# Mixture-of-experts weights as whole 128-wide stationary tiles, with the hidden units dealt out four neighbours to a partition

## What is computed

```python
def moe_swiglu(h, w_router, b_router, w_gate, w_up, w_down):   # 8 experts, D_FF_EXPERT = 3584
    logits = t @ w_router + b_router
    top_v, top_e = lax.top_k(logits, 2)
    gate = softmax(top_v)
    ...
    def one(args):
        xb, e = args
        return (silu(xb @ w_gate[e]) * (xb @ w_up[e])) @ w_down[e]
    out = lax.map(one, (xr, blk_e))
    y = zeros.at[row_tok].add(out * row_g)
```

## Time and profile before

| | |
|---|---|
| median of 3 runs | 2288.18 us (2286.75 to 2290.34) |
| the profiled execution: its own time / its span | 2291.82 us / 2290.1 us |
| PE, DVE, ACT, POOL busy, share of the span | 97%, 39%, 17%, 7% |
| mean granted TensorE clock | 0.985 of full speed |
| read from HBM | 532.94 MB |
| the experts' stretch of PE | 858 to 1743 us |

### The profile page before, as it was taken

One profiled execution on the slowest core, in us unless ns is written; L12 is line 12 of the kernel. 1 busy time (PEld: TensorE's weight loads), 2 busy tenths in 40 slices (PEclk: granted clock), 3 DMA queues, 4 the chain that ended last, 5 costly groups with the idle time before them and its releaser, 6 DMA issues. The chain is left out here.

```text
span 2290.1 us, 49032 instructions
## 1 busy us (share of the span) xinstructions
PE 2216.6 (97%) x22096; PEld 1579.4 (69%) x22096; DVE 883.7 (39%) x1657; ACT 393.3 (17%) x822; POOL 169.4 (7%) x250
## 2 busy tenths in 40 slices
PE   8999999999999999999999999999998999899998
PEld 7699889998689973535353534344446877689997
DVE  2676455452566431010000100111013374768764
ACT  0242311100233320000000010000001342224302
POOL 1000100000000012000000000000001162400000
PEclk9999999999999999999999999999999997899999
DMA  7423354434333377999999999999997211055440
GB/s 248 148 93 130 122 210 158 162 129 166 111 108 123 102 276 281 403 387 393 416 411 417 413 411 414 409 415 408 415 404 261 94 38 39 10 189 187 148 182 20
DMA packets 170559, 540.96 MB, mean 236 GB/s; under 512 B 17068, under 2 KB 35022, under 8 KB 153966
## 3 DMA queue, kind: packets, MB, share of 16 engines
q1 hardware_dynamic: 154144, 528.81, 60.0%
q10 hardware_dynamic: 14622, 4.16, 0.8%
q0 software_dynamic: 1584, 4.85, 0.5%
HBM read 532.94 MB, written 4.85 MB: 235 GB/s over the span
## 5 line engine op out<-in xcount | busy, mean ns | idle before, releaser
L183 PE MATMUL bank<-ring,moe_he 128*32 128x512 f32 (+2 forms) x6144 | 577.7, 537 | 2.8 <-DMA ring<-in_moe_w_up 2.7
L183 PEld LDWEIGHTS bank<-ring,moe_he 128*32 128x32 f32 x6144 | 198.7, 110 | 376.6 <-issue 367.7
L183 PE MATMUL bank<-hT,ring 128*128 128x128 f32 (+1 forms) x1952 | 290.7, 307 | 9.7 <-PEq L932 3.4
L183 PE MATMUL bank<-ring,moe_actT 128*32 128x256 f32 x5352 | 292.3, 379 | 1.3 <-DMA ring<-in_moe_w_down 1.3
L183 PEld LDWEIGHTS bank<-hT,ring 128*128 128x128 f32 x1952 | 263.4, 191 | 33.4 <-issue 8.8
L183 PEld LDWEIGHTS bank<-ring,moe_actT 128*32 128x32 f32 x5352 | 174.1, 110 | 116.9 <-issue 3.9
L2784 DVE TENSOR_TENSOR moe_act<-moe_silu,bank 128x512 f32<-128x512 f32 (+2 forms) x48 | 26.8, 614 | 540.4 <-PE bank L183 540.4
L183 PE MATMUL bank<-ring 128*128 128x128 f32 (+2 forms) x976 | 121.8, 284 | 1.4 <-ACT ring L826 1.4
L183 PEld LDWEIGHTS bank<-ring 128*128 128x128 f32 (+1 forms) x976 | 115.8, 190 | 4.0 <-ACT ring L826 1.8
L183 PE MATMUL bank<-kept,ring 128*128 128x256 f32 (+1 forms) x448 | 96.6, 378 | 6.1 <-PEq L1709 3.0
L183 PEld LDWEIGHTS bank<-kept,ring 128*128 128x128 f32 x448 | 83.2, 198 | 18.5 <-issue 5.4
(11 more groups left out here) (841 smaller groups left out, 2553.1 us busy)
## 6 DMA issues: line engine op xcount, KB each, us to landing
ring<-in_moe_w_down SPq DMA_DIRECT2D x55, 2048.0 KB, 19.1
ring<-in_moe_w_gate SPq DMA_DIRECT2D x32, 2048.0 KB, 23.2
ring<-in_moe_w_up SPq DMA_DIRECT2D x32, 2048.0 KB, 22.8
ring<-in_w_in SPq DMA_DIRECT2D x29, 2048.0 KB, 8.0
ring<-in_moe_w_gate SPq DMA_DIRECT2D x28, 1536.0 KB, 18.1
ring<-in_moe_w_up SPq DMA_DIRECT2D x28, 1536.0 KB, 14.6
ring<-in_w_up SPq DMA_DIRECT2D x10, 2048.0 KB, 11.9
ring<-in_w_out SPq DMA_DIRECT2D x6, 2048.0 KB, 7.9
```

The lines of the kernel that those rows point to most:

```text
L183: ins = pe.matmul(out, lhsT, rhs, start=start, stop=stop, **kw)
```

## The change

It touches only the experts.

- **expand** has the weights as stationary operand, a whole tile of 128 hidden units at a time, and the expert's 96 token slots as moving operand. The result has hidden units on partitions. Blocks are written side by side in a bank, four (`PIECE`) to a bank, so a wave of 16 needs four banks for gate and four for up: 0, 1, 2, 6 and 3, 4, 5, 7.
- The 128 columns of a tile are not neighbours. Of a group of four blocks (512 columns) tile j takes columns j, j + 4, j + 8, ...; so hidden unit 4p + j of the group sits on partition p of block j. A group of three (last expert) has a stride of three.
- **down** loads follow: partition p takes the four neighbouring rows 4p to 4p + 3 of its 512, one run of 16 KB, where it took four rows 128 apart.
- DVE's product goes straight to `moe_actT`; `moe_act` and the 32 x 32 transposes are gone from this path. The two waves are computed piece by piece (4 and 3 pieces instead of 3 and 3).
- **contract** takes 128 columns of `moe_actT` as stationary, from the block's first on: 96 are the block's token slots, the other 32 belong to the next block or are zero padding. 512 down columns move, two matmuls per block. What stands on output partitions 96 to 127 is not used.
- The result is copied as one row per token, sent to DRAM in one transfer of 96 rows, and scattered with 8 whole matmuls instead of 24.
- The spread of expert 0 moves to before and behind its first contract. PE waits for the last result's copies inside the next expert's first k, before the first tile that goes to bank 6.

```diff
-                m.add_slab(("ed", e, w, q // 4), a["moe_w_down"][0, e, f:f + n * P, :].rearrange("(k p) n -> p k n", p=P), n, D)
+                m.add_slab(("ed", e, w, q // 4), a["moe_w_down"][0, e, f:f + n * P, :].rearrange("(p k) n -> p k n", p=P), n, D)
...
-        self.actT = [sb(f"actT{w}", [P, GRP, nb, 32]) for w, (b0, nb) in enumerate(WAVES)]
-        self.ye = sb("ye", [P, GRP, T])
+        self.actT = [sb(f"actT{w}", [P, nb * CAP + P - CAP]) for w, (b0, nb) in enumerate(WAVES)]
+        self.ye = sb("ye", [P, D])
...
-    G, U, DN = m.bank[0:3], m.bank[3:6], m.bank[6:8]
+    G, U, DN = m.bank[0:3] + m.bank[6:7], m.bank[3:6] + m.bank[7:8], m.bank[6:8]
...
-                        for g in range(GRP):
-                            for cg in range(4):
-                                end = k == KD - 1 and g == GRP - 1 and cg == 3
-                                m.mm(pe, banks[g][32 * cg:32 * cg + 32, 0:32 * nb], x.he[:, e % 2, g, k, :],
-                                     chunk(s[:, kk, :], cg, nb), k == 0, k == KD - 1, ready if end else None,
-                                     skip_group_check=True)
+                        for b in range(nb):
+                            if key == "eg" and e and k == 0 and b // PIECE == 3 and b % PIECE == 0:
+                                pe.wait_ge(ye_ready.sem, 2 * e)
+                            c, g = b % PIECE * CAP, b - b % PIECE
+                            n = min(PIECE, nb - g)
+                            cols = s[:, kk, g * P:(g + n) * P].rearrange("p (c n) -> p n c", n=n)[:, b - g, :]
+                            m.mm(pe, banks[b // PIECE][:, c:c + CAP], cols, x.he[:, e % 2, :, k, :],
+                                 k == 0 and c == 0, k == KD - 1, ready if k == KD - 1 and b == nb - 1 else None,
+                                 skip_group_check=True)
...
-                    for g in range(GRP):
-                        for cg in range(4):
-                            first, last = w == 0 and b == 0, w == 1 and b == nb - 1
-                            end = last and g == GRP - 1 and cg == 3
-                            m.mm(pe, DN[g // 2][32 * cg:32 * cg + 32, (g % 2) * T:(g % 2 + 1) * T], x.actT[w][:, g, b, :],
-                                 s[:, b % 4, cg * T:(cg + 1) * T], first and g % 2 == 0, last, d_done if end else None,
-                                 skip_group_check=True)
+                    for h in range(2):
+                        first, last = w == 0 and b == 0, w == 1 and b == nb - 1
+                        m.mm(pe, DN[h][:], x.actT[w][:, b * CAP:b * CAP + P], s[:, b % 4, h * 512:(h + 1) * 512], first, last,
+                             d_done if last and h else None, skip_group_check=True)
...
-                    for g in range(GRP):
-                        v.wait_ge(sg_ready.sem, half * e + GRP * w + g + 1)
-                        v.tensor_tensor(x.act[:, g, 0:32 * nb], x.sg[:, g, 0:32 * nb], U[g][:, 0:32 * nb], ALU.mult)\
-                            .then_inc(mul_done.sem, 1)
-                    for g in range(GRP):
-                        v.wait_ge(mul_done.sem, half * e + GRP * w + g + 1)
-                        v.transpose(x.actT[w][:, g, 0:nb, :].rearrange("p b n -> p (b n)"), x.act[:, g, 0:32 * nb])\
-                            .then_inc(at_ready.sem, 1)
+                    for i, b in enumerate(range(0, nb, PIECE)):
+                        n = min(PIECE, nb - b) * CAP
+                        v.wait_ge(sg_ready.sem, pieces(e, w - 1) + i + 1)
+                        v.tensor_tensor(x.actT[w][:, b * CAP:b * CAP + n], x.silu[:, b:b + n // CAP, :].rearrange("p b n -> p (b n)"),
+                                        U[i][:, 0:n], ALU.mult).then_inc(mul_done.sem, 1)
```

More of the change, by code:

```diff
@@ L2190, in waves, with pieces @@
     return WAVES if e < N_EXPERTS - 1 else (WAVES[0], (16, 11))
+PIECE = 4
+PIECES = sum(-(-nb // PIECE) for _, nb in WAVES)
+def pieces(e, w):
+    return PIECES * e + sum(-(-nb // PIECE) for _, nb in WAVES[:w + 1])
 def plan_experts(m):
@@ L2437, in experts @@
     a = m.a
+    SPREAD = (0, 1, 2, 0, 1, 2, 3, 5)
     def count(eng):
@@ L2505, in scatter, with spread @@
                 pe.wait_ge(selT_ready.sem, 1)
-                for hf in range(2):
-                    for g in range(GRP):
[L2508 to L2519, removed]
+                for c in range(KD):
+                    m.mm(pe, LAST_SC[c // 2][:, c % 2 * T:(c % 2 + 1) * T], x.ye[:, c * P:(c + 1) * P], x.selT[:], True, True,
+                         sc_ready if c == KD - 1 else None)
+            def spread(units):
+                for u in units:
+                    for j in range(2):
+                        m.mm(pe, m.bank[SPREAD[u]][:, j * T:(j + 1) * T], m.onehot[:, u % 4 * 2 + j, :], x.rowT[:, u // 4, :],
+                             True, True, sp_ready if j else None)
             pe.wait_ge(rt.consts.sem, 1)
@@ L2546, in _ @@
                     pe.wait_ge(rt.rb_out.sem, 1)
-                    spread(0)
                 expand("eu", e, 0, U, u_ready)
-                if e == 0:
[L2550 to L2558, removed]
+                pe.wait_ge(sg_ready.sem, pieces(e, 0))
+                expand("eg", e, 1, G, g_ready)
+                pe.wait_ge(mul_done.sem, pieces(e, 0))
+                expand("eu", e, 1, U, u_ready)
+                pe.wait_ge(sg_ready.sem, pieces(e, 1))
+                if e == 0:
+                    spread(range(3))
+                    pe.wait_ge(pads_zero.sem, 3)
+                contract(e, 0)
+                pe.wait_ge(mul_done.sem, pieces(e, 1))
+                if e + 1 < N_EXPERTS:
+                    locate(e + 1)
                 if e == 0:
                     pe.wait_ge(sp_out.sem, 3)
[L2561 to L2572, removed]
+                    spread(range(3, len(SPREAD)))
                 if e == LAST:
                     bring()
-                pe.wait_ge(at_ready.sem, half * e + half)
                 contract(e, 1)
@@ L2594, in _, with spread_out @@
         def _(act):
[L2595 to L2600, removed]
+            def spread_out(u):
+                act.wait_ge(sp_ready.sem, u + 1)
+                e = u % 4 * 2
+                act.activation(x.spread[:, u // 4, e:e + 2, :], m.bank[SPREAD[u]][:].rearrange("p (e n) -> p e n", e=2),
+                               ACT.Copy).then_inc(sp_out.sem, 1)
             for q in range(4):
@@ L2626, in _ @@
                     if e or w:
-                        act.wait_ge(mul_done.sem, half * e + GRP * w)
-                    for g in range(GRP):
-                        act.activation(x.sg[:, g, 0:32 * nb], G[g][:, 0:32 * nb], ACT.Silu).then_inc(sg_ready.sem, 1)
-                    if e == 0:
-                        spread_out(2 * w)
-                        spread_out(2 * w + 1)
+                        act.wait_ge(mul_done.sem, pieces(e, w - 1))
+                    for i, b in enumerate(range(0, nb, PIECE)):
+                        n = min(PIECE, nb - b)
+                        act.activation(x.silu[:, b:b + n, :], G[i][:, 0:n * CAP].rearrange("p (b n) -> p b n", b=n), ACT.Silu)\
+                            .then_inc(sg_ready.sem, 1)
+                if e == 0:
+                    for u in range(len(SPREAD)):
+                        spread_out(u)
                 if e == 1:
@@ L2832, in _ @@
                           allow_small_or_imprecise_dtypes=True), rt.consts)
-            k.step(g.iota(x.slot[:], pattern=[[32, GRP]], base=0, channel_multiplier=1,
-                          allow_small_or_imprecise_dtypes=True))
-            for c in range(1, 4):
-                k.step(g.tensor_scalar(x.slot[32 * c:32 * c + 32, :], x.slot[32 * c:32 * c + 32, :], -32.0 * c, None, ALU.add))
+            k.step(g.memset(x.rowT[:], 0.0), pads_zero)
+            for w, (b0, nb) in enumerate(WAVES):
+                k.step(g.memset(x.actT[w][:, nb * CAP:], 0.0), pads_zero)
+            k.step(g.iota(x.slot[:], pattern=[[0, 1]], base=0, channel_multiplier=1, allow_small_or_imprecise_dtypes=True))
+            k.step(g.memset(x.slot[CAP:P, :], -8.0))
             for i in range(2):
@@ L2882, in _ @@
             m.clear_last(sp)
-            sp.wait_ge(at_ready.sem, half * N_EXPERTS)
+            sp.wait_ge(mul_done.sem, PIECES * N_EXPERTS)
             sp.wait_ge(weighed.sem, 2)
```

51 lines of the change are left out of this document (23 added, 28 removed).

## The result

| | time, us (median) | lowest to highest | ratio to before, 95% interval |
|---|---|---|---|
| before | 2287.47 | 2285.07 to 2290.34 (4 runs) | |
| changed | 3477.41 | 3475.21 to 3478.45 (4 runs) | 1.520, 1.517 to 1.523 |

The account below looks back on a forecast made before the run. TensorE was taken to bound the experts. Expand (796-580.5), contract (384-293.6) and scatter 0.6 sum to 306.5 us, which from the median 2288.2 gives 2595 us; range 2555 to 2675, chance 0.80.

Parts of the forecast that it names:

- What bounds the kernel: In the experts TensorE is busy with nothing idle and sets the pace; transfers, also full, are merely fast enough.
- Expand, whole tiles: Expand: 7136 records at 0.1116 us, paced by the weight load, not the columns: 796 us, against 577.7+2.8 before.
- Contract: Contract: 892 records at 0.431 us, 512 moving columns, load hidden: 384 us, against 292.3+1.3 before.
- Stride: Expand's stationary columns lie four floats apart; price open, from nothing to 0.206 us a load, counted as no cost.
- nearest row: Trace row of a moving operand reading two-float runs four apart: 48 records in 1.59 us, same as with longer runs.
- the farthest price: Upper bound for a strided expand load, from the program's first transposes: 0.206 us each, 0.094 more than counted.
- a stride cost of a tenth: High end of the range: 0.011 us more for each of 7136 expand records, 80 us more, 2675 us.
- Rival 1: The stride costs: each expand load takes up to 0.206 us, expand 1470 us, kernel 3270 us; chance 0.14.
- Down rows, transposes, waits, small: 16 KB down runs, fewer transposes and new waits change nothing; scatter by whole matmuls adds 0.6 us.
- Rival 2: Expand's loads hide completely and only columns count: 578 us, 218 less, kernel 2377 us; chance 0.03, wholly or in part.
- rival 3: A whole-tile f32 matmul is one record, not two; transfers bound the experts, 36 us less, 2252 us; chance 0.03.
- What would show it: Right: experts at clock 1.00, DMA share near 0.75, about 300 GB/s; wrong by stride: expand starts over 0.123 us apart.

Follow-up runs that it names:

- the first experiment: The changed kernel with each tile's 128 gate and up columns side by side and the down rows in their old order; 2589.66 us, ratio 1.131.
- the last experiment: The kernel before, with expand's stationary operand (32 columns of `he`) taken at a stride of four columns; 2293.82 us, ratio 1.0002.

## Why the prediction was right or wrong

*What bounds the kernel.* Right. PE was full before and is full after; more work on PE came through one to one, and transfers, waits, copies and queues played no part. (PE's waits for transfers before were 2.7 us for up and 1.3 for down, not 2.7 in all; it changes nothing.)

*Expand, whole tiles.* Right. The pace of 0.1116 us set by the load, not the columns: 0.1118 in the first experiment, 798.0 us for 796. The estimate of 106.7 ns from the Trainium skill ("TensorE: Matmul & The Clock Gate", "LDWEIGHTS (loading the stationary operand)") is 5% below that; the long streams of the earlier trace rows were the better source. Twice the moving columns showed load and streaming side by side: 192 columns cost no more than 96 while a load of 0.233 lasts.

*Contract.* Right, 385.8 us for 384. In the changed kernel it is 398.5, as the first contract of seven of the eight experts starts at half clock (29.25 to 29.57 us, where the first expert's, behind the spread, takes 27.63). Nothing in the prediction foresaw that.

*Stride.* This is the step that failed: "Its cost is open", then "I take no cost", on the earlier trace rows as nearest row. It cost (1663.8 - 798.0)/7136 = 0.121 us a record, 866 us in expand. The rest of the 888 us between the medians is 12.7 in contract through the clock, and small parts not traced one by one (the spans of the two profiled executions are 882.4 apart). Even the farthest price, 0.206 a record from the earlier trace rows, was below the 0.233 measured, and the range ended at a stride cost of a tenth, 2675 us.

Two errors lie in it. The nearest row was no neighbour. The earlier trace rows reads runs of two floats four apart, that is two elements of each 16 bytes. By that count it is the case of a stride of two (1.05 for a load, 1.06 for a stream), though no run tried this very pattern. The changed kernel takes one of each 16 bytes, and for that the trace had no row. Besides, its records stream 32 columns in 0.033 us, too short to show much. And the range's upper end was a guess ("a tenth") where a mechanism had been named. Rival 1 stated it: each element on a new line. It had a chance of 0.14 and is the case that came, in its mechanism; its price of up to 3270 us was too low as well, since it came from loads that have nothing to do with a stride. Looking back, I would give it half the chance: the change does exactly what that rule of the Trainium skill speaks against, and no row spoke to it.

*Down rows, transposes, waits, small.* Right: the down rows are worth nothing (1.1316 against 1.1308), and PE waits for no transfer or copy.

*Rival 2* (loads hide) and *rival 3* (one record per matmul) are out: 7136 records, and 0.112 us at best.

*What would show it.* "Starts over 0.123 apart" was the sign of a wrong stride, and it is what the trace shows. The clock of 1.00 and 300 GB/s hold only without the stride (1.00 and 307; the DMA share there is 0.86, not 0.75).

## What to carry to other kernels

Look at the innermost step of both operands that TensorE reads from SBUF: for f32 in these runs, every second float cost 5 to 6% over neighbours and every fourth 2.1 times as much, in loads and in streams alike, and every third 1.6 times in a load. A relayout that gives one long run per partition is no gain if the matmul then has to pick its columns apart: here the long runs alone were worth nothing, and the stride cost 866 us. If a stride can't be avoided, put it on an operand whose read is covered by a longer one, as the last experiment does; undoing it in the DMA was not tried. And when a term's price is open and a rule names its mechanism, give that rule the chance that the absence of any row leaves it, and ask of the nearest row whether it has the property in question.

## What the runs showed that was not expected

- The load at a stride of four costs the same at both clock levels: 10 records per 2 us at 1.00 and at 0.50, and 209.15 us per expert in the changed kernel against 209.16 with twice the moving columns and a full clock. At a stride of three it does not: 0.175 us at full clock, 0.211 at half. What sets the 0.211 was not shown: no run has tiles of neighbouring columns with 96 moving columns at half clock. The nearest row, outside the experts, is 14 records with 128 moving columns in 3.14 us at a clock of 0.50 (`cffn_xg`, 3216.61 us in the changed kernel), some 0.213 each, but there streaming and load can't be told apart.
- The granted clock fell to 1.2 GHz while PE was busy without a gap. It fell with slow loads and 96 moving columns a record (mean over the span 0.753, and 0.750 at a stride of eight), and did not with 192 columns at the same pace (0.992), nor with 96 columns at 0.112 (0.989). PE's busy time as the profile counts it was 100% of the experts' stretches in all of them.
- A stream at a stride of four takes 2.09 to 2.11 times its time whether one stream runs or four in strips. Elements of another size were not tried, in loads or in streams.
